# Encoder trunk on one core: transposed feed-forward rows moved into the first group, and the norm behind attention moved into the output projection

## What is computed

```python
x = x + rms_norm(mix, norm_mix_post)
h = rms_norm(x, norm_ffn_pre)
f = square(relu(h @ w_ff1)) @ w_ff2        # w_ff1: 1024 x 4096, w_ff2: 4096 x 1024
x = x + rms_norm(f, norm_ffn_post)
```

## Time and profile before

| | us |
|---|---|
| median of 3 runs | 4654.06 (4652.25 to 4656.37) |
| the profiled execution | 4658.73 |
| its span in the trace | 4656.9 |
| PE busy | 4203.9 (90% of the span) |
| DVE, ACT, POOL busy | 2206.1, 1402.1, 1157.4 |
| mean granted TensorE clock | 0.937 of full speed |

### The profile page before, as it was taken

How to read it: one execution, slowest core, us unless ns; L and a number is a source line. 1 busy time by engine, 2 the same in 40 slices (tenths; PEclk the granted TensorE clock), 3 DMA queues, 4 the chain that set the end, 5 groups by cost and what they waited for, 6 DMA issues and landing times. The chain is left out here.

```text
span 4656.9 us, 63032 instructions
## 1 busy us (share of the span) xinstructions
PE 4203.9 (90%) x24160; PEld 3636.8 (78%) x24160; DVE 2206.1 (47%) x3171; ACT 1402.1 (30%) x2266; POOL 1157.4 (25%) x647
## 2 busy tenths in 40 slices
PE   7999686899999999769999999789998789999997
PEld 6889565888888888658888888668886678888885
DVE  5643344555555555653333343546662334333344
ACT  4321463333333333241111111325542411111111
POOL 1120134333333333131111111203430221111112
PEclk9999778999999999879999999889999899999998
DMA  4221583111111110231111111210001221111112
GB/s 121 75 91 65 165 287 121 51 47 46 46 46 46 46 46 19 95 120 48 36 45 36 36 36 36 90 34 7 7 1 41 91 64 36 36 37 44 36 36 90
DMA packets 204977, 285.97 MB, mean 61 GB/s; under 512 B 31152, under 2 KB 148208, under 8 KB 204800
## 3 DMA queue, kind: packets, MB, share of 16 engines
q1 hardware_dynamic: 204800, 283.40, 18.7%
HBM read 205.37 MB, written 77.99 MB: 61 GB/s over the span
## 5 line engine op out<-in xcount | busy, mean ns | idle before, releaser
L619 DVE TENSOR_TENSOR top_acc<-top_acc,ffn_bank 128x512 f32<-128x512 f32 x640 | 439.7, 687 | 400.1 <-PE ffn_bank L110 400.1
L108 PE MATMUL ffn_bank<-hT_ffn_high,ffn_w_high 128*128 128x512 f32 (+1 forms) x1536 | 544.9, 355 | 29.4 <-DVE ffn_w_low L596 29.4
L109 PE MATMUL ffn_bank<-hT_ffn_low,ffn_w_high 128*128 128x512 f32 (+1 forms) x1536 | 544.6, 355 | 0.0
L110 PE MATMUL ffn_bank<-hT_ffn_high,ffn_w_low 128*128 128x512 f32 (+1 forms) x1536 | 544.5, 354 | 0.0
L108 PE MATMUL ffn_bank<-ffn_w_high,ffn_f_high 128*128 128x512 f32 x1280 | 498.3, 389 | 0.0
L109 PE MATMUL ffn_bank<-ffn_w_low,ffn_f_high 128*128 128x512 f32 x1280 | 498.3, 389 | 0.0
L110 PE MATMUL ffn_bank<-ffn_w_high,ffn_f_low 128*128 128x512 f32 x1280 | 497.9, 389 | 0.0
L611 DVE TENSOR_TENSOR ffn_square<-ffn_relu 128x512 f32<-128x512 f32 (+1 forms) x192 | 146.5, 763 | 661.9 <-ACT ffn_relu L564 661.9
L108 PEld LDWEIGHTS ffn_bank<-hT_ffn_high,ffn_w_high 128*128 128x128 f32 x1536 | 291.3, 190 | 71.6 <-issue 30.2
L109 PEld LDWEIGHTS ffn_bank<-hT_ffn_low,ffn_w_high 128*128 128x128 f32 x1536 | 291.3, 190 | 41.5
L110 PEld LDWEIGHTS ffn_bank<-hT_ffn_high,ffn_w_low 128*128 128x128 f32 x1536 | 291.3, 190 | 40.1
(11 more groups left out here) (414 smaller groups left out, 9065.3 us busy)
## 6 DMA issues: line engine op xcount, KB each, us to landing
ffn_w_raw<-in_w_ff SPq DMA_DIRECT2D x64, 1024.0 KB, 5.3
s_x<-top_acc SPq DMA_DIRECT2D x30, 512.0 KB, 5.1
norm_x_old<-s_x SPq DMA_DIRECT2D x30, 512.0 KB, 4.4
project_w_raw<-in_w_in_even SPq DMA_DIRECT2D x27, 512.0 KB, 5.0
s_tm_both<-prepare_tb SPq DMA_DIRECT2D x20, 512.0 KB, 7.3
s_fm_dir<-prepare_fd SPq DMA_DIRECT2D x20, 512.0 KB, 6.1
scan_tb<-s_tm_both SPq DMA_DIRECT2D x20, 512.0 KB, 3.6
scan_fb<-s_fm_both SPq DMA_DIRECT2D x20, 512.0 KB, 4.3
```

Of the source, the lines that this page charges most:

```text
L108: pe.matmul(out, stationary[0], moving[0], start=start, stop=False)
L109: pe.matmul(out, stationary[0], moving[1], start=False, stop=False)
L110: return pe.matmul(out, stationary[1], moving[0], start=False, stop=stop)
L619: dve.tensor_tensor(a, a, bank[4 + u % 4][:, :], ALU.add).then_inc(added, 1)
```

## The change

Three edits.

1. Both feed-forwards get `h` as rows in `acc` and turn it themselves. The first of the 16 groups is written out ahead of the loop: four tiles are turned before it, and tiles 4 to 9 two at a time inside its first three up units, after the second k step. The turned tiles go through the PSUM banks of the down units. The first group's down units are copied into `acc` in place of added, so the clearing of `acc` is gone. POOL makes the low part of w1 for every group. The norm in front writes `h` over `acc` (`rows_only`), has no PE transposes, and keeps the new x in five buffers with a store semaphore each.
2. The norm in front of the second feed-forward has no stage any more. `project_latent` does it tile by tile while PE works on the next tile. Its gains come by two DMAs into SBUF.
3. The first weights of each feed-forward are asked for in the stage in front (`FirstWeights`).

```diff
-def residual_norm(nc, E, x_src, x_dst, hT, ident, gain_rows, X, g_post, g_pre):
+def residual_norm(nc, E, x_src, x_dst, hT, ident, gain_rows, X, g_post, g_pre, up=None):
...
+    rows_only = pre and hT is None
+    AHEAD = 5 if rows_only else 3
+    BEHIND = 2
...
+    slot_stored = [E.sem(f"slot_stored{j}") for j in range(AHEAD)]
+
+    def x_new(t):
+        return x_old[t % AHEAD][:, :] if rows_only else X[:, t, :]
...
+            if up is not None:
+                sp.dma_start(up.w1_raw[:, :, :], up.w1v[:, :, 0:up.n]).then_inc(up.w1_loaded, 16)
+                sp.dma_start(up.w2_raw[:, :, :], up.w2v[:, 0:up.n // P, :]).then_inc(up.w2_loaded, 16)
+            if rows_only:
+                for t in range(TILES):
+                    sp.wait_ge(x_updated, t + 1)
+                    sp.dma_start(of(x_dst, t), x_new(t)).then_inc(slot_stored[t % AHEAD], 16)
+                    n = t - BEHIND
+                    if n >= 0 and n + AHEAD < TILES:
+                        sp.wait_ge(slot_stored[n % AHEAD], 16 * (n // AHEAD) + 16)
+                        sp.wait_ge(h_ready, n + 1)
+                        load(n + AHEAD)
+                for j in range(AHEAD):
+                    sp.wait_ge(slot_stored[j], 16 * len(range(j, TILES, AHEAD)))
...
+                if rows_only:
+                    dve.scalar_tensor_tensor(X[:, t, :], x_new(t), col(rc2, t), gpre[:, :], ALU.mult, ALU.mult).then_inc(h_ready, 1)
+                    return
...
-def feed_forward(nc, E, hT, acc, w1, w2):
+def feed_forward(nc, E, rows, ident, hT, acc, up):
...
-    bank = E.banks(8)
+    bank = E.banks(4)
+    down = [E.stack.enter_context(nc.psum_tensor(f"{E.tag}_down{j}", [P, 2, 512], F32)) for j in range(2)]
...
+    BEFORE_FIRST = 4
+    TURNS = ((4, 5), (6, 7), (8, 9))
...
         @block.tensor
-            with pe.Fori(0, GROUPS) as i:
+            def turn(t):
+                if t >= 2:
+                    pe.wait_ge(row_low, t - 1)
+                for k in range(KB):
+                    last = pe.transpose(down[t % 2][:, k // 4, (k % 4) * P:(k % 4 + 1) * P], rows[:, t, k * P:(k + 1) * P], ident[:, :])
+                last.then_inc(turned, 1)
+
+            def group(i, first):
...
+                    if first:
+                        pe.wait_ge(row_low, (t0 + n) // P)
                     for k in range(KB):
                         last = product(...)
+                        if first and k == 1 and u < len(TURNS):
+                            for t in TURNS[u]:
+                                turn(t)
...
+            for t in range(BEFORE_FIRST):
+                turn(t)
+            group(0, True)
+            with pe.Fori(0, GROUPS - 1) as i:
+                group(i + 1, False)
 
         @block.scalar
+            def row(t):
+                act.wait_ge(turned, t + 1)
+                act.activation(hT[0][part(t)], down[t % 2][:, :, :].rearrange("p a (k n) -> p (a k) n", n=P), ACT.Copy).then_inc(row_high, 1)
...
+            act.wait_ge(w1_loaded, 16)
+            act.activation(w1_sb[0][:, :, :], w1_raw[:, :, :], ACT.Copy).then_inc(w1_high, 1)
+            for t in range(BEFORE_FIRST):
+                row(t)
+            group(0, True, True)
...
         @block.gpsimd
-            pool.memset(acc[:, :, :], 0.0).then_inc(zeroed, 1)
...
         @block.vector
+            def row(t):
+                dve.wait_ge(row_high, t + 1)
+                dve.tensor_tensor(hT[1][part(t)], down[t % 2][:, :, :].rearrange("p a (k n) -> p (a k) n", n=P),
+                                  hT[0][part(t)].bitcast(F32), ALU.subtract).then_inc(row_low, 1)
...
+                    if first:
+                        dve.tensor_copy(a, out_of(u)).then_inc(added, 1)
...
-def project_latent(nc, E, ins, ident, mix, w_out):
+def project_latent(nc, E, ins, ident, mix, w_out, x, g_post, g_pre, up):
...
+            sp.dma_start(gpost[:, :], g_post.partition_broadcast(P)).then_inc(gains, 16)
+            sp.dma_start(gpre[:, :], g_pre.partition_broadcast(P)).then_inc(gains, 16)
+            for t in range(RING):
+                load(t)
+            sp.dma_start(up.w1_raw[:, :, :], up.w1v[:, :, 0:up.n]).then_inc(up.w1_loaded, 16)
+            sp.dma_start(up.w2_raw[:, :, :], up.w2v[:, 0:up.n // P, :]).then_inc(up.w2_loaded, 16)
+            for t in range(TILES):
+                sp.wait_ge(x_updated, t + 1)
+                sp.dma_start(x_of(t), x_row[t % RING][:, :]).then_inc(stored[t % RING], 16)
...
         @block.scalar
             for t in range(TILES):
-                act.wait_ge(multiplied, t + 1)
-                act.activation(two(mix[:, t, :]), ps[2 + t % 2][:, :, :], ACT.Copy).then_inc(done, 1)
+                mix_root_of(t)
                 if t + 2 < TILES:
                     high(t + 2)
+                x_root_of(t)
+
+        @block.gpsimd
+            for t in range(TILES):
+                pool.wait_ge(loaded[t % RING], 16 * (t // RING) + 16)
+                pool.wait_ge(mix_scaled, t + 1)
+                pool.tensor_tensor(x_row[t % RING][:, :], mix[:, t, :], x_row[t % RING][:, :], ALU.add).then_inc(x_updated, 1)
 
         @block.vector
+            for t in range(TILES):
+                mixer(t)
+                if t + 2 < TILES:
+                    low(t + 2)
+                rows(t)
...
-            phase("norm3", residual_norm, x_mid, x_mid, hT, ident, gain_rows, acc, gain("norm_mix_post", 1), gain("norm_ffn_pre", 1))
-            phase("ffn1", feed_forward, hT, acc, ins["w_ff1"][1], ins["w_ff2"][1])
+            phase("ffn1", feed_forward, acc, ident, hT, acc, up)
```

More of the change, by code:

```diff
@@ L200, in _ @@
                     x_root_of(t + 1)
-                if pre and t >= 0:
+                if hT is not None and t >= 0:
                     high(t)
@@ L240, in _ @@
                     rows(t + 1)
-                if pre and t >= 0:
+                if hT is not None and t >= 0:
                     low(t)
+            if pre and hT is None:
+                dve.wait_ge(h_ready, TILES)
         @block.tensor
@@ L251, in _ @@
                 last.then_inc(gains, 1)
-            if pre:
+            if hT is not None:
                 for t in range(TILES):
@@ L561, in group @@
                     n = PIECES[q][1]
-                    act.wait_ge(up_product, UP * i + u + 1)
-                    act.wait_ge(squared, UP * i + u + 1)
+                    if first and u < len(TURNS):
+                        for t in TURNS[u]:
+                            row(t)
+                    act.wait_ge(up_product, UP * i + (u + 1))
+                    act.wait_ge(squared, UP * i + (u + 1))
                     act.activation(relu[u % 2][:, 0:n], bank[u % 4][:, 0:n], ACT.Relu).then_inc(relu_done, 1)
@@ L608, in _ @@
                     n = PIECES[q][1]
-                    dve.wait_ge(relu_done, UP * i + u + 1 + 4)
-                    dve.wait_ge(f_low, UP * i + u + 1)
+                    if first and u < len(TURNS):
+                        for t in TURNS[u]:
+                            row(t)
+                    dve.wait_ge(relu_done, UP * i + (u + 1 + 4))
+                    dve.wait_ge(f_low, UP * i + (u + 1))
                     dve.tensor_tensor(square[u % 2][:, 0:n], relu[u % 2][:, 0:n], relu[u % 2][:, 0:n],
@@ L616, in _ @@
                 for u in range(DOWN):
-                    dve.wait_ge(down_product, DOWN * i + u + 1)
+                    dve.wait_ge(down_product, DOWN * i + (u + 1))
                     a = acc[:, u // 2, (u % 2) * 512:(u % 2 + 1) * 512]
-                    dve.tensor_tensor(a, a, bank[4 + u % 4][:, :], ALU.add).then_inc(added, 1)
-                dve.wait_ge(added, DOWN * i + DOWN + 4)
+                    if first:
+                        dve.tensor_copy(a, out_of(u)).then_inc(added, 1)
+                    else:
+                        dve.tensor_tensor(a, a, out_of(u), ALU.add).then_inc(added, 1)
+                dve.wait_ge(added, DOWN * i + (DOWN + 4))
+            dve.sem_inc(added, 4)
+            for t in range(BEFORE_FIRST):
+                row(t)
+            group(0, True)
+            with dve.Fori(0, GROUPS - 1) as i:
+                group(i + 1, False)
 def prepare_tokens(nc, E, ins, ident, eps, gates, rates, conv_fm, shift_fm, fm_both, fm_dir, tm_both, tm_dir):
@@ L2859, in _ @@
                 if t >= 2:
-                    pe.wait_ge(done, t - 1)
+                    pe.wait_ge(mix_scaled, t - 1)
                 for half in range(2):
@@ L2901, in _ @@
                 dve.tensor_tensor(two(w[1][:, h, :]), ps[h % 2][:, :, :], two(w[0][:, h, :]).bitcast(F32), ALU.subtract).then_inc(w_low, 1)
-            for t in range(2, TILES):
-                low(t)
-            dve.wait_ge(low_done, TILES)
+            dve.wait_ge(gains, 32)
+            for t in range(TILES):
[3 more added lines that the diff above has]
+                rows(t)
+            dve.wait_ge(h_ready, TILES)
 def clear_semaphores(nc, sems):
@@ L2982, in program @@
         with ExitStack() as wide:
```

(7 more changed lines are left out.)

145 lines of the change are left out of this document (98 added, 47 removed).

## The result

| | before | after |
|---|---|---|
| median of the runs, us | 4653.2 | 4613.7 (4 runs, 4603.1 to 4618.7) |
| profiled execution, us | 4658.7 | 4612.1 |
| its span, us | 4656.9 | 4610.3 |
| ratio of the times, 95% interval | | 0.9912 [0.9897, 0.9927] |

The forecast was 4612, the range 4605 to 4624. The change is faster by 39.5 us.

What follows compares the result with a forecast made beforehand. PE, busy 90% of the span, was taken as the bound, except in norm stages, bound by a ring through four engines. -8.2 + 4.3 + 5.0 - 43.9 + 0.3 = -42.5 us, against 4654.06 giving 4612; range 4605 to 4624.

Steps and rivals of the forecast that it cites:

- Part 1: norm1 without turns: shorter ring and last tile, less clears and late transfers, -8.2 us in all.
- The ring's 6.92 us: norm1: with low off DVE, the mixer two tiles on starts at +6.92 instead of +8.05 us.
- The 0.5 put on late transfers: norm1: 0.5 us allowed for load 5 landing at about 23 us when POOL wants it at 22.7.
- Part 2: Start of each feed-forward: early weights, turns ahead and inside group 0; +4.3 us for ffn0, +5.0 for ffn1.
- Lost at half clock after that: Feed-forward, behind the first product: slow clock costs nothing or 2.2 us (six matmuls, one turn); 1.1 taken.
- Part 3: norm3 inside out1: the norm hides under PE except the last tile, so ffn1 starts earlier, -43.9 us.
- part 4: Three other norm stages clear three more semaphores each, +0.3 us.
- A: Group 0 of each feed-forward: units with turns wait for copy and low, 6.8 us each, time 4625; 12%.
- B: norm1: stores and loads set the pace at 4.03 us a tile as before, time 4618; 10%.
- C: out1: DVE and POOL shut each other out, chain 12.1 us against PE's 10.88 a tile, time 4622; 4%.
- D: Group 0 of both feed-forwards runs at half clock, 102 us more, slower than before at 4714; 3%.
- E: out1: the norm is not hidden but paid tile by tile, so nothing of note changes, 4654; 1%.

Runs made afterwards that it cites:

- e11: The changed kernel itself, unedited, measured once more on another occasion: 4616.7 us, ratio 0.9908 to the kernel before.
- e1: Layer 0 of the change alone, with out1, norm3 and ffn1 as in the kernel before: 4652.7 us, ratio 0.9995.
- e4: Changed kernel with gains, x rows and feed-forward weights in out1 asked for only after all projection weights landed: 4615.3 us.
- e12: e10 with DVE's low of tile t+2 placed behind rows of tile t in out1: 4604.6 us.
- e7: Changed kernel with e4's wait, and rows 2 and 3 turned into the up products' banks, so four buffers for the first turns: 4608.3 us.
- e3: Changed kernel with both weight loads moved back to the feed-forward's start: 4627.1 us.
- e9: e7 with turns 4 and 5 moved ahead of the first unit, so six turns come before it: 4606.1 us.
- e6: Changed kernel with eight rows turned in norm1 and w1 split there in four pieces by ACT and POOL: 4612.6 us.
- e10: e6's layer 0 with ACT's w1 pieces one tile earlier and POOL taking each one tile later, plus e9's layer 1: 4603.5 us.

## Why the prediction was right

**Part 1, -8.2: measured -8.2** (52.3 to 44.1). The ring's 6.92 us for two tiles came as 6.91 and 6.97. The 0.5 put on late transfers was not needed for them (under 0.1). But the close, from the end of the last `rows` at 2071.51 to the first turn at 2073.71, took 2.2 where 1.53 and 0.2 were meant. The forecast read a clear's price as its 30 ns; the step between two is 57 ns, so seven more cost 0.4. Another 0.2 passes ahead of the first clear, from a cause that stays open. The two small errors cancelled, and that is luck.

**Part 2, +4.3 and +5.0: measured +6.4 and +6.5 in the first profile, +4.4 and +5.4 in e11.** The term that was mis-sized is "Lost at half clock after that [...] I take 1.1". From first product to first product, every group but group 0 lasts 54.74 us, before and after. Group 0 lasted 62.94 in the first profile, 8.2 more, against 6.0 + 1.1 in the sum. The turns are less than 6.0: 5.45 at full clock (e1). That leaves 2.75 for the slow clock, above even the 2.2 that the forecast gave as its worst case (six matmuls and one turn). It was six matmuls (1.2) and two turns in 3.16 instead of 1.67 (1.5). In e11 group 0 cost 1.1 less. In `ffn0` the close is the rest of the miss: from the end of the last accumulation on DVE (starts 2968.41, 0.69 long) to the first load of `norm2` (2971.54) pass 2.4 us, and before the change 1.5. Sixteen clears take 1.33 us there and fourteen took 0.74, of which only 0.1 is two more clears at 57 ns; another 0.3 passes ahead of the first clear. All eight profiles with 16 clears in `ffn0` have the 1.33, so it is no scatter; why they are slow there stays open. In `ffn1` the close grew by 0.1 only (1.5 to 1.6).

**Part 3, -43.9: measured -42.5, and -44.7 in e11.** The tail was 10.9 instead of 10.5: 16 more clears cost 0.9 us and not 0.5. "The weight loads and the x rows queue behind the projection's own weights [...]: nothing" failed by a little in the first profile, where the first weights landed late. Its first product came 0.95 us later than in the kernel before. In e11 it came 1.2 us earlier, because the clock rose earlier (e4).

**Sum.** From `norm1` to the end of the program the changed kernel's two profiles are 39.8 and 41.1 us shorter than the kernel before (2620.5); the forecast was 42.5. Parts 1 to 3 alone measured -37.8 and -43.2. The stages that the change hardly touches (`norm2`, `latent`, `attend`, `norm4`; part 4 gave the norms some tenths) were 2.0 us shorter in the first profile and 2.0 longer in e11. So single profiles can't test the sum more finely than 2 us. The medians stand 39.5 apart, 3.0 less than forecast. The profiled execution came out at 4612.1 where 4616.2 was meant, because this execution also reached `norm1` 6.8 us sooner, which e1 and e11 (2036.2 and 2041.1) show to be chance. So it is in part luck that the median fits within 2 us.

**Rivals.** A, stalls in group 0: false, PE is busy for all of it, as the stretch from the first product to the next group shows:

```profile
2084.20:2147.10 62.90, 62.90 (x312) 53.84 (x313) 27.10 (x37) 14.08 (x20) 9.15 (x2) 0.95 0.13 41
```

B, transfers set norm1's pace: one wait and no loss, at 285 GB/s.

C: `low` does slow POOL's add, and its price is nothing. The add takes 3.24 us beside `low` and 2.39 with `low` moved away (e12). The forecast's sign for it, a `low` of 2 us or more, did not come: `low` starts first and keeps its 1.22 us, and the add alone is longer. PE is the bound there, busy for 109.40 of 109.40 us, and the last tile has no `low`. That the two engines shut each other out was the author's reading; the runs show the durations, not the cause.

D, a group at half clock: false, the clock is up 5.8 us after the first product; where it fell back behind a pause of the turns, as in e7 and e11, it was up again after 3.4 us. It fell back behind pauses of 2.7 us (e7) and 2.5 us (e11), and not behind 2.5 us in e1. The size, 2.75 us, is near the forecast's 2.2 and not that of the rival. E: false.

The change pays in one place. The stage that was merged into a projection bound by PE gave 42 to 45 us, less the 5.4 to 6.5 by which `ffn1` grew. Moving the turns out of `norm1` gave 8 and took 3 to 6 back in `ffn0` (2.8 in e1, 4.4 in e11, 6.4 in the first profile). Without the early request layer 0 would have lost: 947.1 us in e3 against 943.8 before.

## What to carry to other kernels

A chain of small steps on ACT, DVE and POOL belongs beside a stage that PE bounds: here the products of `out1` took 109.0 us with the norm beside them and without it. Work of PE moved from a stage where PE was half idle into one where PE is the bound was paid here: six turns cost group 0 5.45 us at full clock (e1). At the start of a PE stage, count the pauses ahead of the first product as well as its time: two useful turns put into e7's pause of 2.7 us (e9) bought their own 1.7 us, and with the pause at 1.0 us the clock stayed up, 1.4 us more. When a helper's piece is put into a ring of engines, let it be made one step before it is wanted: in e6 POOL stood 3.0 us before each piece and its adds came 6.6 us apart, in e10 no piece waited and they came 4.2 apart (7 us of layer 0).
